# Where VectorE's addition of a down block stands among the low parts of the weights, in both SwiGLU layers

## The reference, cut to what matters

```python
def swiglu(x, w_gu, w_d):
    gate, up = jnp.split(x @ w_gu, 2, axis=-1)
    return (jax.nn.silu(gate) * up) @ w_d

for l in range(DEPTH):                       # DEPTH = 2
    h = mixer_even(...) if l % 2 == 0 else mixer_odd(...)
    x = layer_norm(ALPHA * x + h, ln1_g[l], ln1_b[l])
    x = layer_norm(ALPHA * x + swiglu(x, ffn_wgu[l], ffn_wd[l]), ln2_g[l], ln2_b[l])
```

## Time and profile before

| | |
|---|---|
| three runs | 3451.91, 3452.29, 3452.88 us (median 3452.29) |
| span of the profiled execution, first to last instruction | 3451.0 us |
| TensorE matmul rows busy | 3435.9 us (100% of the span) |
| TensorE weight loads busy | 2803.5 us (81%) |
| VectorE busy | 1940.5 us (56%) |
| ScalarE busy | 1608.0 us (47%) |
| GpSimd busy | 302.7 us (9%) |
| DMA engines, mean share | 5 to 7 tenths in nearly every slice |
| granted TensorE clock | 0.999 of full |

### The profile page before, as it was taken

How to read it: one execution, slowest core, us unless ns; L and a number is a source line. 1 busy time by engine, 2 the same in 40 slices (tenths; PEclk the granted TensorE clock), 3 DMA queues, 4 the chain that set the end, 5 groups by cost and what they waited for, 6 DMA issues and landing times.

```text
span 3451.0 us, 42740 instructions
## 1 busy us (share of the span) xinstructions
PE 3435.9 (100%) x15844; PEld 2803.5 (81%) x15844; DVE 1940.5 (56%) x2315; ACT 1608.0 (47%) x2063; POOL 302.7 (9%) x418
## 2 busy tenths in 40 slices
PE   9999999999999999999999999999999999999999
PEld 8788878888888888777888878888888788888887
DVE  4544575555555665667556544567544845555556
ACT  5444444444444455454444434446556644444443
POOL 0000010000000000001343303000380000000000
PEclk9999999999999999999999999999999999999999
DMA  7556665556556555456556657665654556655554
GB/s 247 166 171 177 202 203 188 183 183 200 190 179 201 159 172 159 128 194 166 189 178 193 196 160 211 204 199 168 186 174 150 167 185 191 192 186 186 189 187 143
DMA packets 333317, 630.11 MB, mean 183 GB/s; under 512 B 33181, under 2 KB 36097, under 8 KB 331649
## 3 DMA queue, kind: packets, MB, share of 16 engines
q1 hardware_dynamic: 326272, 603.20, 55.8%
q0 software_dynamic: 6768, 25.05, 2.3%
q10 hardware_dynamic: 144, 0.07, 0.0%
HBM read 624.86 MB, written 2.33 MB: 182 GB/s over the span
## 4 chain that ended last, share of the span: by engine, by line
PE 97%; DVE 2%; ACT 1%; issue 0%; DMA 0%; SPq 0%; DVEq 0%; ACTq 0%
PE psum L268 29%; PE psum L270 28%; PE psum L269 28%; PE psum L322 3%; PE psum L600 1%; PE psum L602 1%; PE psum L601 1%; PE psum L937 1%; PE psum L950 0%; PE psum L3135 0%; PE psum L518 0%; PE psum L516 0%; PE psum L517 0%; DVE weights_lo L230 0%; PE psum L3155 0%
## 5 line engine op out<-in xcount | busy, mean ns | idle before, releaser
L230 DVE TENSOR_TENSOR weights_lo<-weights_raw,weights_hi 128x1024 fp32r<-128x1024 f32 (+1 forms) x1139 | 1394.4, 1237 | 1153.3 <-ACT weights_hi L217 1152.6
L217 ACT CAST weights_hi<-weights_raw 128x1024 fp32r<-128x1024 f32 (+1 forms) x1139 | 1192.7, 1050 | 1667.1 <-PE psum L270 1655.5
L268 PE MATMUL psum<-weights_hi,act_hi 128*128 128x512 f32 x3048 | 1211.7, 398 | 0.1
L270 PE MATMUL psum<-weights_hi,act_lo 128*128 128x512 f32 x3048 | 1189.9, 390 | 0.0
L269 PE MATMUL psum<-weights_lo,act_hi 128*128 128x512 f32 x3048 | 1188.0, 390 | 0.0
L270 PEld LDWEIGHTS psum<-weights_hi,act_lo 128*128 128x128 f32 x3048 | 572.5, 188 | 122.8
L268 PEld LDWEIGHTS psum<-weights_hi,act_hi 128*128 128x128 f32 x3048 | 572.9, 188 | 121.4 <-issue 8.9
L269 PEld LDWEIGHTS psum<-weights_lo,act_hi 128*128 128x128 f32 x3048 | 573.5, 188 | 113.0
L268 PE MATMUL psum<-weights_hi,hid_hi 128*128 128x512 f32 x1320 | 523.6, 397 | 0.0
L270 PE MATMUL psum<-weights_hi,hid_lo 128*128 128x512 f32 x1320 | 514.5, 390 | 0.0
L269 PE MATMUL psum<-weights_lo,hid_hi 128*128 128x512 f32 x1320 | 514.1, 389 | 0.0
(11 more groups left out here) (452 smaller groups left out, 1932.9 us busy)
## 6 DMA issues: line engine op xcount, KB each, us to landing
weights_raw<-in_ffn_wgu SPq DMA_DIRECT2D x344, 512.0 KB, 4.4
weights_raw<-in_w_ff SPq DMA_DIRECT2D x252, 512.0 KB, 3.9
weights_raw<-in_ffn_wd SPq DMA_DIRECT2D x176, 512.0 KB, 3.7
weights_raw<-in_even_w_in SPq DMA_DIRECT2D x120, 512.0 KB, 3.6
weights_raw<-in_w_in SPq DMA_DIRECT2D x64, 512.0 KB, 3.7
weights_raw<-in_odd_w_in SPq DMA_DIRECT2D x60, 512.0 KB, 3.7
weights_raw<-in_odd_w_o SPq DMA_DIRECT2D x32, 512.0 KB, 3.8
weights_raw<-in_w_out SPq DMA_DIRECT2D x32, 512.0 KB, 3.9
```

The costliest lines, as they stand in the source:

```text
L217: nc.scalar.copy(w_hi[:, u % SPLIT_SLOTS, done:size], raw[:, u % RAW_SLOTS, done:size]).then_inc(hi_ready, 1)
L230: nc.vector.tensor_tensor(w_lo[:, u % SPLIT_SLOTS, done:size], raw[:, u % RAW_SLOTS, done:size], w_hi[:, u % SPLIT_SLOTS, done:size].bitca ...
L268: nc.tensor.matmul(o, ah, wh, start=(k + j == 0), stop=False)
L270: last = nc.tensor.matmul(o, al, wh, start=False, stop=(k + j == kts - 1))
```

## The change

`block_split` gets an argument `at`, the number of the low part ahead of which the extra work stands; without it nothing changes. The four down blocks of a step pass 2. Where a down block has two units, the number 2 isn't reached and the extra work stands behind both low parts. In the last dense layer a down block has four units and `(4 + 1) // 2` is 2 already.

```diff
-    def block_split(one, eng, c, kts, cols, between=None):
+    def block_split(one, eng, c, kts, cols, between=None, at=None):
         us = units_of(kts, cols)
+        at = (len(us) + 1) // 2 if at is None else at
         for j, (_, nk) in enumerate(us):
-            if between is not None and j == (len(us) + 1) // 2:
+            if between is not None and j == at:
                 between()
                 between = None
             one(eng, c, nk * cols)
@@ in step, on VectorE
                 for j in range(4):
-                    block_split(unit_lo, dve, c, kts, BLK, out_)
+                    block_split(unit_lo, dve, c, kts, BLK, out_, 2)
```

## The result

| | before | changed |
|---|---|---|
| median of 9 runs each | 3452.29 us | 3443.67 us |
| lowest to highest | 3451.31 to 3453.39 | 3443.18 to 3445.18 |
| span of the profiled execution | 3451.0 us | 3441.9 us |

The ratio is 0.9977, with a 95% interval of 0.9969 to 0.9985: 8.6 us less, where 7.5 were forecast. The forecast of 3444.8 us is 1.1 us high, and the range from 3443.0 to 3447.3 us holds the median. The prediction set the line of a clear difference at 0.2%. The median is beyond it at 0.25%, but the interval begins at 0.15%, so nine runs don't settle on which side of the line the change lies.

A forecast was written before the change was run, and what follows sets the result against it. TensorE was taken to bound the kernel, losing time where weight loads wait for VectorE's low part. Gains of 7.02 and 0.50 us, 7.52 together, with moved work at 0, took 3452.3 to 3444.8 us; range 3443.0 to 3447.3.

The forecast's parts named there:

- What bounds the kernel, and where: TensorE sets the end; its hidden-tile weight loads wait for VectorE's low part 75 times, 17.5 us, at second down units.
- the rival that trusted them: Matmul rows are right and the waits lie beside them: nothing gained, 3452.3 us; chance 3%.
- What each costs: SwiGLU down blocks: unit pace against undisturbed 2.72 us gives 7.52 us lost by TensorE, all to be regained.
- the 18 stretches: Eight down units each, in steps without transposes in the stretch: 398.70 us together against 391.68 undisturbed, 7.02 us lost.
- the two long units of each last step: Units of 2.80 to 2.89 us in each SwiGLU layer's last step, against 2.72: 0.50 us lost over both layers.
- The rival that gives back all idle time: All idle time of the hidden weight loads, 14.5 us, comes back: 3437.8 us; chance of more than the sum 3%.
- the one with half of the excess left: Excess of two-unit blocks only partly the low part's; with half left 3448.5 us; chance of part left 7%.
- The weight-load share: Loads' busy share, 79.9% in the stretches against 82.8% in the last dense layer: gain of 13.8 us, not taken.
- Moved work without cost: Second low parts move ahead of the taking out; additions, last steps, SyncE's queue and last dense layer cost 0.
- The room of the bank pair: Bank pair wanted one block of 5.44 us after release, free after 1.3: 4.1 us of room for the addition.
- The slower rival: Addition caught behind a late second low part, bank pair stays taken, TensorE stops: 16 us more, 3460.8 us; chance 3%.
- the base of the sum: Profiled execution's span of 3451.0 us, with the runs' median 1.3 us above it: 3452.3 us before the gain.

The follow-up runs named there:

- the two layers apart: Two runs, the addition moved in the first or second SwiGLU layer alone, against the kernel before: 3447.33 us (3.88 less) and 3447.59 us (3.62 less).
- the comparison with 33 runs of the kernel before: Changed kernel again, no edit, 11 runs, against the kernel before on the same chip: 3443.84 us against 3451.21, ratio 0.9980.
- the sums alone: Only a step's three down-block additions moved, the up block's taking out left between low parts, against the kernel before: 3446.84 us, 0.9989.

## Why the prediction was right

**What bounds the kernel, and where.** Right. The waits of the weight loads on the low part vanished, all 75. None of it was to be seen in the idle time of the matmul rows, so the rival that trusted them is out.

**What each costs.** Right in method and size: the pace of the units, not the idle time of the loads. Forecast 7.52 us; measured 7.10 in the 18 stretches and the two long units of each last step gone, 7.50 for the two layers apart, 7.4 in the comparison with 33 runs of the kernel before. The rival that gives back all idle time (14.5 us) is out, and so is the one with half of the excess left: nothing above 2.72 us a unit is left in the 18 stretches.

**The weight-load share.** Sizing by the share gave 13.8 us, and I didn't take it because overlapping loads are counted once. After the change the share is 324.25 / 391.60 = 82.8%, just that of the last dense layer. The Trainium skill (Perfetto Trace Analysis, Identifying the Most-Contended Engine) names this share as a measure of how near TensorE is to its limit. The trace agrees as to the sign, as it rose when the waits went. But the busy time rose too, by 5.55 us or 0.08 us in each of 72 places, near the overlap of 0.09 us at the place that was read. The share said that there was room; the length had to come from the starts.

**Moved work without cost.** Right: the second low part came at 617.42 (I had said 617.7), 4.4 us ahead of the taking out. The room of the bank pair, 4.1 us by my reading, held with 2.2 us of it used (3.5 less the 1.3 of the taking out) and was overrun with 4.9.

**The slower rival.** Its mechanism exists, though it was brought about by order and not by a late landing, which no run tested: with five low parts ahead the bank pair comes late, and the time rises by 51.5 us. The Trainium skill's strict order of VectorE's queue (PSUM — Partial Sum Buffer, Engine vs sequencer instructions) is seen at work there, and in the last dense layer, where a taking out caught the freeing of a transpose buffer. The change stays on the free side of it.

**What was off: the base of the sum.** The forecast for the profiled execution was 3443.5 us and its span is 3441.9, so 1.6 us less. The prediction set the profiled execution's time as its span plus 1.3 us, from the median of three runs. The changed kernel's runs lie 1.8 us above their spans (3443.67 to 3441.9). By the same distance the profiled execution of the kernel before took about 3452.8 us, with 1.6 us of slow clock in it that the mean of 0.999 hid and that I didn't look for. Nine runs of the kernel before had a median between its two groups, nine of the changed kernel had one in the lower group. That is where the 1.1 us between 7.5 and 8.6 come from, as far as the later jobs show; in the largest one the difference is 7.4 us. The gain was right by its mechanism. That the median came out within 1.1 us of the forecast was partly luck, since either median could have fallen in its other group.

## What to carry to other kernels

When one engine is busy for 100% of the span, look for its lost time in the pace: take the same work at two places, one undisturbed, and subtract. In a hand-written order put what is wanted soon ahead of what waits for something, and work out for the waiting instruction how long its result has room; here it could end 3.5 us behind its block for nothing, and at 6.2 us it cost 1.26 us a place. And before a difference of 0.05% is explained, look at the single times: if they fall in groups, a median of a few runs moves by the distance of the groups.

## What wasn't expected of the hardware

Waits of the weight loads for 3 us cost more than themselves: behind them the granted clock read 0.57 to 0.64 over stretches of 4 us, and a place priced at 2.6 us cost 4.1. It fell 66 times behind 80 such waits. Waits of 0.2 us never did that; the granted clock was 1.00 in all 18 stretches of either kernel. Nor did the 40 waits of 1.35 us on average with five low parts ahead: the granted clock read 1.00 in those down blocks too.

The clock also fell to 1.2 GHz for some 3.4 us without a wait of that kind, behind 22 small matmuls in 2.9 us, in one of two traces of the same program and not in the other. It costs 1.6 us. Of the 12 traces that have the whole run of 22, three have the fall (the kernel before, the sums alone, five low parts), and in each it begins 2.9 to 3.6 us after the first of them, at 1439.9, 1437.4 and 1460.4. What decides it stays open: the shift in time alone doesn't, and with the run of small matmuls cut to 16 two of ten times were still in the upper group.
